# Dilated attention: one copy moved ahead of an exponential, and the last head's query norms taken one row earlier

## The reference, cut to what matters

```python
q = rms_norm(q, q_norm_g) * (HEAD_DIM ** -0.5)        # 24 heads of 128: 3 groups x 8
for g, (window, d) in enumerate(DILATED_GROUPS):      # dilation 1, 4, 16
    o, lse = dilated_group_attn(q[:, :, hs], kb, vb, slopes[hs], window, d)
alpha = jax.nn.softmax(jnp.stack(lses), axis=0)       # the groups are weighed together
o = jnp.sum(alpha[..., None] * jnp.stack(outs), axis=0)
y = o.reshape(bsz, s, B_WIDTH) * jax.nn.silu(z)
return x + gate * (y @ w_out)
```

## Time and profile before

| | |
|---|---|
| median of 3 runs | 2057.77 us (2057.09 to 2062.7) |
| the profiled execution | 2057.85 us |
| its span, first to last instruction | 2056.2 us |
| mean granted clock of PE | 0.969 of full speed |
| PE busy | 1917.6 us (93%) |
| DVE busy | 1138.5 us (55%) |
| ACT busy | 766.1 us (37%) |
| chain that ended last | PE 85%, DVE 9%, ACT 3%, issue 2%, DMA 1% |
| the changed stage | from about 538 to 834 us of the span |

### The profile page before, as it was taken

How to read it: one execution, slowest core, us unless ns; L and a number is a source line. 1 busy time by engine, 2 the same in 40 slices (tenths; PEclk the granted TensorE clock), 3 DMA queues, 4 the chain that set the end, 5 groups by cost and what they waited for, 6 DMA issues and landing times.

```text
span 2056.2 us, 23357 instructions
## 1 busy us (share of the span) xinstructions
PE 1917.6 (93%) x8598; PEld 1545.2 (75%) x8598; DVE 1138.5 (55%) x1565; ACT 766.1 (37%) x995; POOL 39.1 (2%) x96
## 2 busy tenths in 40 slices
PE   4999999989999997999999996999999979999997
PEld 4788888867788886778888874776667758888885
DVE  6346666468366666454334456598665464433455
ACT  3455554233355544322322233233442342222232
POOL 1000000000000000000000000000000000000000
PEclk8999999989999998999999998999999999999997
DMA  8445565412222211233343241232111223234321
GB/s 310 152 125 173 174 180 159 143 62 76 64 66 56 68 61 44 62 102 85 90 112 97 64 125 41 82 103 62 42 62 62 87 57 100 75 99 114 94 71 60
DMA packets 288195, 198.42 MB, mean 96 GB/s; under 512 B 6562, under 2 KB 275188, under 8 KB 287092
## 3 DMA queue, kind: packets, MB, share of 16 engines
q1 hardware_dynamic: 279568, 163.63, 27.6%
q0 software_dynamic: 8064, 33.56, 4.6%
q10 hardware_dynamic: 484, 0.16, 0.0%
HBM read 195.21 MB, written 2.11 MB: 96 GB/s over the span
## 4 chain that ended last, share of the span: by engine, by line
PE 85%; DVE 9%; ACT 3%; issue 2%; DMA 1%; DVEq 0%; POOL 0%; ACTq 0%; POOLq 0%
PE acc L596 19%; PE acc L598 19%; PE acc L597 19%; PE acc L786 3%; PE acc L788 3%; PE acc L787 3%; PE acc L1061 1%; PE acc L1062 1%; DVE s_rstd L1616 1%; PE acc L1063 1%; DMA s_ada_w<-in_a_ada_w 1%; ACT s_w_high L1143 1%; PE sc L1022 1%; PE ob L837 1%; DVE s_xT L2063 1%
## 5 line engine op out<-in xcount | busy, mean ns | idle before, releaser
L1578 DVE TENSOR_TENSOR s_w_low<-s_raw,s_w_high 128x2048 fp32r<-128x2048 f32 x159 | 364.4, 2292 | 324.6 <-ACT s_w_high L1143 324.6
L596 PE MATMUL acc<-s_h_high,s_w_high 128*128 128x512 f32 x1184 | 469.4, 396 | 28.4 <-DVE s_h_low L1625 9.0
L597 PE MATMUL acc<-s_h_low,s_w_high 128*128 128x512 f32 x1184 | 462.6, 391 | 0.0
L598 PE MATMUL acc<-s_h_high,s_w_low 128*128 128x512 f32 x1184 | 462.4, 391 | 0.0
L1143 ACT ACTIVATE s_w_high<-s_raw 128x2048 fp32r<-128x2048 f32 x159 | 303.0, 1905 | 23.7 <-PE sc L681 18.1
L596 PEld LDWEIGHTS acc<-s_h_high,s_w_high 128*128 128x128 f32 x1184 | 223.0, 188 | 83.6 <-issue 32.2
L597 PEld LDWEIGHTS acc<-s_h_low,s_w_high 128*128 128x128 f32 x1184 | 223.2, 189 | 46.7 <-issue 2.0
L598 PEld LDWEIGHTS acc<-s_h_high,s_w_low 128*128 128x128 f32 x1184 | 223.1, 188 | 46.5
L596 PE MATMUL acc<-s_b_high,s_w_high 128*128 128x512 f32 x576 | 229.0, 398 | 10.0 <-DVE s_b_low L1627 5.8
L597 PE MATMUL acc<-s_b_low,s_w_high 128*128 128x512 f32 x576 | 226.1, 393 | 0.0
L598 PE MATMUL acc<-s_b_high,s_w_low 128*128 128x512 f32 x576 | 225.9, 392 | 0.0
(11 more groups left out here) (312 smaller groups left out, 2418.4 us busy)
## 6 DMA issues: line engine op xcount, KB each, us to landing
s_raw<-in_a_w_in SPq DMA_DIRECT2D x48, 512.0 KB, 5.0
s_raw<-in_ffn_w_gate SPq DMA_DIRECT2D x44, 512.0 KB, 3.9
s_raw<-in_ffn_w_up SPq DMA_DIRECT2D x44, 512.0 KB, 5.1
s_raw<-in_w_in SPq DMA_DIRECT2D x36, 512.0 KB, 4.0
s_raw<-in_b_w_in SPq DMA_DIRECT2D x32, 512.0 KB, 5.2
s_ada_w<-in_b_ada_w POOLq DMA_DIRECT2D x24, 512.0 KB, 5.0
s_raw<-in_ffn_w_down SPq DMA_DIRECT2D x32, 384.0 KB, 3.9
s_raw<-in_ffn_w_down SPq DMA_DIRECT2D x32, 320.0 KB, 3.7
```

The source lines that it names most:

```text
L596: pe.matmul(acc[b][:, :], w_high[:, o:o + P], hi, start=(k == 0), stop=False, skip_group_check=grouped)
L597: pe.matmul(acc[b][:, :], w_high[:, o:o + P], lo, start=False, stop=False, skip_group_check=grouped)
L598: mm = pe.matmul(acc[b][:, :], w_low[:, o:o + P], hi, start=False, stop=(k == nk - 1), skip_group_check=grouped)
L1578: dve.tensor_tensor(w_low[:, w], raw[:, w], w_high[:, w].bitcast(F32), ALU.subtract).then_inc(w_ready, 1)
```

## The change

1. In ACT's list, `store_g12(s-2, 3)` moves from behind the exponential and `leave` of step (s, 0) to directly behind `store_g0(s-2, 3)`, ahead of the exponential. This holds for s from 2 to 8.
2. The query norms of head 7 (`square_sums` on PE, the mean and the reciprocal on DVE, the root on ACT) move from step (7, 3) to step (7, 2). The other heads keep theirs in step n = 3.
3. Behind PE's loop, the first half of tile 31 moves ahead of `scores` of head 7's row 0.

```diff
+def norm_row(s):
+
+    return 3 if s < NQ - 1 else 2
...
                     project(s, n, 0)
-                    if n == 3:
+                    if n == norm_row(s):
                         square_sums(s)
...
             a, j = NQ - 1, (NQ - 1) % 2
+            project(NQ, 0, 0)
             scores(a, j, 1, 0)
-            project(NQ, 0, 0)
             turn(a - 1, 3)
...
-                    if s < NQ and n == 3:
+                    if s < NQ and n == norm_row(s):
                         act.wait_ge(qms_ready, s + 1)
                         act.activation(tiny[:, Q_RT:Q_RT + 12], tiny[:, Q_MS:Q_MS + 12], ACT.Sqrt).then_inc(q_root, 1)
                     if s > 0 and n > 0:
                         store_g0(s - 1, n - 1)
                     elif s > 1:
                         store_g0(s - 2, 3)
+                        store_g12(s - 2, 3)
...
                     if s > 0 and n > 0:
                         store_g12(s - 1, n - 1)
-                    elif s > 1:
-                        store_g12(s - 2, 3)
...
-                    if s < NQ and n == 3:
+                    if s < NQ and n == norm_row(s):
                         dve.wait_ge(qsq_summed, s + 1)
...
-                    if s < NQ and n == 3:
+                    if s < NQ and n == norm_row(s):
                         dve.wait_ge(q_root, s + 1)
                         dve.reciprocal(tiny[:, Q_R + 12 * (s % 2):Q_R + 12 * (s % 2) + 12], tiny[:, Q_RT:Q_RT + 12])\
                            .then_inc(qr_ready, 1)
```

## The result

| | before | after |
|---|---|---|
| median | 2056.85 us (2053.85 to 2064.24, 15 runs) | 2065.81 us (2062.16 to 2068.91, 15 runs) |
| ratio of the times, 95% interval | | 1.0038 (1.0026 to 1.0049) |
| the profiled execution, its span | 2057.85, 2056.2 us | 2068.71, 2067.0 us |
| mean granted clock of PE | 0.969 | 0.964 |

The changed kernel is slower by 9.0 us (by the interval of the ratio, 5.3 to 10.1), where 1.3 us faster was forecast; the time lies above the range, which ended at 2060.5. The mean clock of all its 15 executions lies between 0.963 and 0.966. The trace of before is one of the first kind.

The account below looks back on a forecast made before the run. PE, busy for 93% of the span, was taken as the bound. Terms of -6.2 us at full clock and +1.7, +1.6 and +1.6 us for the clock summed to -1.3 us, 2056.5 us; range 2051.6 to 2060.5 us.

Parts of the forecast that it names:

- issue: Ahead of `weighted(0)`: the wait table's word for PE's 1.09 us gap, whose releaser was forecast to be ACT's copy.
- the term of -4.6 for five heads: Heads 2 to 6: the moved copy gains 0.92 us a head, with a new wait of 0.2 to 0.3 us.
- I take one: +1.6 (ends 0 and +8): Sums of heads 2 to 6: one clock fall of 1.6 us expected, out of 0 to 5 possible.
- the nearest row: Clock behind new waits: judged by the profile row with the most similar wait, such as head 1's 1.00 us.
- the three heads with a fall: Heads 0, 1 and 7 before the change: their sums are followed by a stretch at lower clock.
- one observation rather than five: The five heads without a fall before: they repeat at a nearly fixed distance, so count once.
- the price of a fall: Half tile behind head 1's sums: 4.42 us in place of 2.84, so 1.6 us.
- the second rival: Sums of heads 2 to 7: waits pull the clock down in nearly every head, +3.5 to +5.1 us; chance 0.12.
- -0.8 - 0.85 + 1.7 + 1.6: Head 7 and tail: row 3's turn earlier, shorter wait to `weighted(6)`, slow scores of row 0, fall behind head 7's sums.
- two terms of the clock: Head 7: row 0's scores at the lower clock behind idleness, +1.7 us; a fall behind the sums, +1.6 us.
- The third rival: The copy is not what `weighted` waits for; moved norms alone cost about +3 us, 2060.9 us; chance 0.04.
- The rule on the loads: Head 7, row 2's exponential: new table load costs 1.28 us, without the skill's extra drain of some 1.38 us.

Follow-up runs that it names:

- e5: Kernel before with only the copy moved, plus two more dense products a head in heads 2 to 6: 2059.45 us, ratio 1.0017.
- e2: Kernel before with only head 7's norms moved earlier and tile 31's first half ahead of the scores, copy unmoved: 2062.83 us, ratio 1.0027.
- e3: The whole change, with the sums of heads 0 to 6 in three pieces of 8 matmuls: 2049.45 us, ratio 0.9956 to before.
- e4: Kernel before with only the copy moved and the sums of all heads in three pieces: 2045.78 us, ratio 0.9944.
- e8: e4 with ACT's and DVE's steps on the first output chunk taken behind head 6's last row: 2041.35 us, ratio 0.9917 to before.
- e9: Kernel before with the sums in three pieces and nothing else: 2059.44 us, ratio 1.0015.
- e10: The whole change, with sums of heads 0 to 6 in pieces and first output chunk's steps behind head 6's last row: 2046.26 us, ratio 0.9944 to before.
- e6: Kernel before with only the copy moved, plus four more dense products a head in heads 2 to 6: 2055.21 us, ratio 0.9993.
- e1: Kernel before with only the copy moved, norms and order behind the loop unchanged: 2062.88 us, ratio 1.0025.

## Why the prediction was wrong

**The copy.** Right: L1316 directly behind L1305, no idle time ahead of L858, and "issue" was the copy. My reason for that was weaker than it read: 0.10 us is not what a semaphore costs elsewhere, PE's waits with a named releaser in this stage start 0.05 us behind its end, and only the seven gaps that the view calls "issue" have 0.10. A head gained 0.77 us and not 0.92, since the new wait is 0.32 us, and the gap of 1.09 less 0.32 is what is left; the 0.92 and a wait of 0.2 to 0.3 didn't go together in my text either. So the term of -4.6 for five heads was -3.8. The six closed gaps of the result's account, 6 x 0.77, come to -4.6 too, but the sixth is head 7's; that the two numbers agree is luck.

**Sums of heads 2 to 6: the step that failed.** "I take one: +1.6 (ends 0 and +8)". It was 9.6 us: four falls, two of them of double length, beyond the end of 8 that I had given. Three errors are in it. The first is the choice of the nearest row by the length of the wait; e5 has falls with no wait at all, and so had head 0 in the trace of before, which I had counted among the three heads with a fall and yet passed over when I tied the falls to a wait. The second is that I called the five unharmed heads "one observation rather than five" and then still weighed it as evidence for the burst's harmlessness. What they showed was that the clock held at one distance in one execution, and the distance is what the change alters. The third is the price of a fall, which came from a single row; a fall can be double. With 9.6 in place of 1.6 the sum is +6.7; the second rival, to which I gave 0.12, named falls in nearly every head and gave 2063, though it too put them down to the waits.

**Head 7 and the tail.** Behind the sums of head 6 I had -0.8 - 0.85 + 1.7 + 1.6 = +1.65. Measured from these sums to `weighted(7)`, 87.93 us in place of 83.03, it is +4.9, of which 3.2 are head 6's own fall: +1.7. That it agrees so well is luck, as two terms of the clock were wrong and cancel. The timeline of after, beside the earlier trace rows:

```profile
779.19 4.50 PE L842 MATMUL ob<-s_ones,s_q_sq 128*128 128x1 f32 x24 [1.85 <-ACT s_q_sq L1336]
...
788.79 0.38 ACT L1305 ACTIVATE s_pT<-tr 128x256 f32<-128x256 f32 x1 [4.64 <-PE tr L827]
...
789.19 1.28 ACT L1361 ACT_TABLE_LOAD   x1
790.49 0.61 ACT L1361 ACTIVATE s_s_row<-s_s_row,s_tiny 128x384 f32<-128x384 f32 x1
...
793.00 0.37 ACT L1316 ACTIVATE s_pT<-misc 96x256 f32<-96x256 f32 x1
...
795.20 2.29 DVE L1582 TENSOR_TENSOR s_w_low<-s_raw,s_w_high 128x2048 fp32r<-128x2048 f32 x1 [3.36 <-ACT s_w_high L1148]
...
797.79 2.02 DVE L1921 SCALAR_TENSOR_TENSOR s_s_row<-sc,s_tiny,s_bias 32x32 f32<-32x32 f32 x8
...
799.95 0.67 PE L807 MATMUL sc<-s_kT,s_qT 128*128 128x256 f32 x2 [1.76 <-DVE s_s_row L1921]
...
802.25 0.27 PE L827 MATMUL tr<-s_ident,s_s_row 128*128 128x128 f32 x1
```

The chain is the predicted one: the sums wait 1.85 us (1.8); the new load stands ahead of the exponential, which starts 1.70 behind the copy (0.38 + 1.28); from it to L1316 2.51 (2.51), to the low part 2.20 more (2.20), to the end of `tops` 4.61 (4.69); scores of row 0 wait for L1921. The two terms of the clock: the scores of row 0 ran at the full clock (2.30 us to the turn), with 1.76 us of idleness ahead of them, since the half tile stood in the wait: 0 for my +1.7. The half tile itself ran at the lower clock in part, 793.59 to 797.99 us, but it only filled a wait with that. The sums took 4.50 and the half tile behind them 4.18 (788.37 - 784.19), so this fall too was a double one, +3.2 for my +1.6. The third rival put the moved norms alone at about +3; e2 measured +7.0, and what I had missed there is the gap ahead of `weighted(6)`, 3.26 us, which the copy behind the late exponential makes.

**The rule on the loads.** The exponential starts 0.02 us behind the load's end (789.19 + 1.28 = 790.47), as in the earlier trace rows. The drain of some 1.38 us for each change of table set that the Trainium skill, "ScalarE: Activation LUTs", "What ACT_TABLE_LOAD costs", counts does not show on this path. It was right to go by the row.

**What stays open.** Why the traced execution of before, with 34.3 us from head to head, is free of falls and those with 33.6 and 35.2 us are not, and what makes some executions of before run at the lower mean clock: the runs show that it is so, and no more. Which heads have falls in a given execution, since only one of each kernel is traced. And whether the two lengths of the stage from 1275 us on are chance alone.

## What to carry to other kernels

An idle gap on an engine that is busy for 93% is worth its length only if the clock holds without it: in a loop of equal rounds, look at the granted clock behind each run of small matmuls before you price an edit that changes the round's length, and take "no fall in n rounds of one trace" for one observation; the mean clock of every execution is worth a look too. First break the bursts up, then close the gaps: here the copy cost 7 us with the sums in one piece and brought 13.7 us with them in three. And before splitting, look at which engine's chain sets the round's length, since splitting by itself made the round 0.5 us longer.

## What was not expected of the hardware

- 24 matmuls of one column, 0.11 us from one to the next, can be followed by a fall of PE's clock to 1.2 GHz with no idle time before or behind them (e5, granted clock 0.76 and 0.88 over 14 us with PE busy for 14.00 of them). In pieces of 8, with 3 us between them, there was no fall in any of the heads 2 to 6 of five kernels (e3, e4, e8, e9, e10).
- The Trainium skill, "TensorE: Matmul & The Clock Gate", section "Why this matters for your kernels", ties drops of the clock in the middle of a kernel to idle gaps of PE between its bursts. In e5 there is no such gap from 590 to 720 us, and three falls; without the bursts in one piece (e4) there is neither.
- More work was faster: e6 adds 4.5 us of matmuls to e1 and takes 7.7 us less.
- Behind the sums of heads 2 to 6 a fall came in two sizes, 1.6 and 3.2 us (granted clock 0.88 and 0.76 over 14 us).
- One and the same kernel ran at two mean clocks: 59 of 80 executions of before at 0.968 to 0.972 (2052 to 2058 us), 21 at 0.961 to 0.967 (2061 to 2073 us).
